# Differential heads' norm factors: from transposes in PSUM to broadcast loads through DRAM, with the normalisation moved into the forget attention

## What is computed

```python
def rmsnorm(x, g):
    xf = x.astype(jnp.float32)
    y = xf * lax.rsqrt(jnp.mean(xf * xf, axis=-1, keepdims=True) + EPS)
    return (y * g.astype(jnp.float32)).astype(x.dtype)
...
        ad = pd[:, :, 0] - lam * pd[:, :, 1]
        od = jnp.einsum('bhqk,bkhe->bqhe', ad.astype(dv.dtype), dv)
        od = rmsnorm(od, subln_g) * (1.0 - lambda_init)
        sf = jnp.einsum('bqhd,bkhd->bhqk', qf, fk).astype(jnp.float32) * (FOX_HEAD_DIM ** -0.5)
        sf = sf + jnp.transpose(cq, (0, 2, 1))[..., :, None] - cum_k[..., None, :]
        pf = jax.nn.softmax(jnp.where(causal, sf, NEG), axis=-1)
        of = jnp.einsum('bhqk,bkhd->bqhd', pf.astype(fv.dtype), fv)
        return jnp.concatenate([od.reshape(B, Q_BLOCK, DIFF_WIDTH),
                                of.reshape(B, Q_BLOCK, FOX_WIDTH)], axis=-1)
```

## Time and profile before

| | us |
|---|---|
| median of three runs | 1284.31 |
| the profiled execution's own time | 1284.02 |
| its span | 1282.2 |
| TensorE busy | 1268.9 (99%) |
| VectorE busy | 766.5 (60%) |
| ScalarE busy | 549.3 (43%) |
| GpSimd busy | 32.5 (3%) |
| chain that ended last | TensorE 95%, VectorE 3%, ScalarE 1%, issue 1% |

### The profile page before, as it was taken

The page is one execution under the profiler, slowest core; times in us unless marked ns, Lnnn a source line. Parts: engine busy times, 40 slices in busy tenths (PEclk is TensorE's granted clock), DMA queues, the critical chain, the costliest instruction groups (busy, mean ns, idle before and its releaser), DMA issues.

```text
span 1282.2 us, 17439 instructions
## 1 busy us (share of the span) xinstructions
PE 1268.9 (99%) x6386; PEld 1072.7 (84%) x6386; DVE 766.5 (60%) x1250; ACT 549.3 (43%) x921; POOL 32.5 (3%) x42
## 2 busy tenths in 40 slices
PE   9999999999999999999999999999999999999997
PEld 7887888988888888888888888888988888888886
DVE  6777895655444443323685896898868422455334
ACT  6656865433222223232564655667443222222221
POOL 0010000000000000000000000000000000000002
PEclk9999999999999999999999999999999999999999
DMA  5232113122223223332333323423122322222332
GB/s 199 85 130 83 34 36 130 34 76 89 98 98 98 98 90 124 102 111 98 99 104 110 99 83 93 114 79 112 50 66 85 112 92 92 96 98 98 99 99 82
DMA packets 37563, 120.97 MB, mean 94 GB/s; under 512 B 4600, under 2 KB 6776, under 8 KB 37504
## 3 DMA queue, kind: packets, MB, share of 16 engines
q1 hardware_dynamic: 35888, 116.93, 28.3%
q0 software_dynamic: 896, 2.64, 0.7%
q10 hardware_dynamic: 720, 0.59, 0.1%
HBM read 112.79 MB, written 2.11 MB: 90 GB/s over the span
## 4 chain that ended last, share of the span: by engine, by line
PE 95%; DVE 3%; ACT 1%; issue 1%; DVEq 0%; ACTq 0%
PE bank L902 29%; PE bank L903 29%; PE bank L904 29%; PE bank L1003 2%; PE bank L1096 1%; DVE arena L2157 1%; PE bank L1423 1%; PE bank L1125 0%; PE bank L1141 0%; PE bank L1383 0%; PE bank L1382 0%; DVE tiles L2154 0%; PE bank L1033 0%; PE bank L1073 0%; DVE tiles L2157 0%
## 5 line engine op out<-in xcount | busy, mean ns | idle before, releaser
L2154 DVE TENSOR_TENSOR w_lo<-raw_slab,w_hi 128x1024 fp32r<-128x1024 f32 (+1 forms) x199 | 243.6, 1224 | 269.1 <-ACT w_hi L1541 264.6
L902 PE MATMUL bank<-u_hi,w_hi 128*128 128x512 f32 x824 | 322.8, 392 | 0.0
L904 PE MATMUL bank<-u_hi,w_lo 128*128 128x512 f32 x824 | 321.0, 390 | 0.0
L903 PE MATMUL bank<-u_lo,w_hi 128*128 128x512 f32 x824 | 320.9, 389 | 0.0
L1541 ACT ACTIVATE w_hi<-raw_slab 128x1024 fp32r<-128x1024 f32 x197 | 207.7, 1054 | 183.8 <-PE bank L904 181.3
L902 PE MATMUL bank<-arena,w_hi 128*128 128x512 f32 (+1 forms) x692 | 260.9, 377 | 0.0
L903 PE MATMUL bank<-arena,w_hi 128*128 128x512 f32 (+1 forms) x692 | 259.3, 375 | 0.0
L904 PE MATMUL bank<-arena,w_lo 128*128 128x512 f32 (+1 forms) x692 | 259.3, 375 | 0.0
L904 PEld LDWEIGHTS bank<-u_hi,w_lo 128*128 128x128 f32 x824 | 154.7, 188 | 32.4
L902 PEld LDWEIGHTS bank<-u_hi,w_hi 128*128 128x128 f32 x824 | 154.7, 188 | 31.7 <-issue 0.9
L903 PEld LDWEIGHTS bank<-u_lo,w_hi 128*128 128x128 f32 x824 | 154.8, 188 | 30.7
(11 more groups left out here) (275 smaller groups left out, 1451.5 us busy)
## 6 DMA issues: line engine op xcount, KB each, us to landing
raw_slab<-in_stream SPq DMA_DIRECT2D x197, 512.0 KB, 3.3
aside_raw<-in_stream SPq DMA_DIRECT2D x8, 512.0 KB, 5.2
arena<-arena SPq DMA_DIRECT2D x32, 128.0 KB, 2.3
residual<-in_xT SPq DMA_DIRECT2D x8, 256.0 KB, 5.6
out_hT<-residual SPq DMA_DIRECT2D x12, 128.0 KB, 1.8
arena<-forget_rows SPq DMA_DIRECT2D x8, 128.0 KB, 2.4
raw_slab<-in_stream SPq DMA_DIRECT2D x2, 256.0 KB, 3.3
early<-decay_rows POOLq DMA_DIRECT2D x2, 256.0 KB, 3.8
```

Of the source, the lines that this page charges most:

```text
L902: pe.matmul(o, ws[0], xs[0], start=first, stop=False)
L903: pe.matmul(o, ws[0], xs[1], start=False, stop=False)
L904: return pe.matmul(o, ws[1], xs[0], start=False, stop=last)
L2154: return nc.vector.tensor_tensor(o, a, b, op)
```

## The change

One transpose of the whole 128x16 tile of factors by the identity gives 16x128 in bank 0 (`df_factor_rows`), after k-step 3 and no longer after k-step 4. ScalarE copies the rows to SBUF and stores them in DRAM (`factor_rows`, 8 KB), splits a slab, waits for the store, and issues four loads that each bring one head's row of 512 factors into all 128 partitions (256 KB each, into the tiles `MO`+h, free there). The normalisations, the high parts and the low parts leave the place between the slabs and go to the heads' work of the forget attention: `df_normed(h)` in step 6+h, ScalarE's `df_mix_hi(h)` in step 7+h, `mix_low` of head h in step 8+h. The normalisation works in place in `kept`, and so no longer waits for a temporary tile.

```diff
-DF_SPREAD_BANKS = (0, 1, 5, 7)
+DF_ROWS_BANK, DF_NORMED = 0, 6
...
+    use("df_rows", DF_ROWS_BANK, (sem.spread_ready, n + 1), (sem.df_rows, 1))
...
-            def df_spreads():
-
+            def df_factor_rows():
+
+                o = claim("df_rows")
                 pe.wait_ge(sem.rstd_done, NORM_NO["df"] + 1)
-                for h in range(DF_H):
-                    head_spread("df", h, sem.df_spread)
+                every = rstds[:, RSTD0["df"]:RSTD0["df"] + DF_H].rearrange("p h n -> p (h n)")
+                pe.transpose(o[0:DF_H * ST, 0:P], every, ident).then_inc(sem.spread_ready, 1)
...
-                    elif k == 4:
-                        df_spreads()
+                    elif k == 3:
+                        df_factor_rows()
...
+            rows = tiles[0:DF_H * ST, SQ, 0:P]
+            nc.scalar.activation(rows, full(act, "df_rows")[0:DF_H * ST, 0:P], ACT.Copy).then_inc(sem.df_rows, 1)
+            act.wait_ge(sem.df_rows, 1)
+            act.dma_start(factor_rows.rearrange("h (n p) -> (h n) p", p=P), rows).then_inc(sem.df_rows_stored, 16)
             slab_hi(SLAB0["fv"] + 2)
+            act.wait_ge(sem.df_rows_stored, 16)
             for h in range(DF_H):
+                act.dma_start(t(MO + h), factor_rows[h].partition_broadcast(P)).then_inc(sem.df_factors_loaded, 16)
+            slab_hi(SLAB0["fv"] + 3)
+
+            def df_mix_hi(h):
                 act.wait_ge(sem.head_normed, ML_H + h + 1)
-                nc.scalar.activation(ar(MIX_HI + h), t(TMP + h % 2), ACT.Copy).then_inc(sem.mix_hi, 1)
-            slab_hi(SLAB0["fv"] + 3)
+                nc.scalar.activation(ar(MIX_HI + h), kept[:, h], ACT.Copy).then_inc(sem.mix_hi, 1)
...
+                if 0 <= step - DF_NORMED - 1 < DF_H:
+                    df_mix_hi(step - DF_NORMED - 1)
...
+            slab_lo(SLAB0["fv"] + 3)
+
             def df_normed(h):
-                factor = full(dve, ("spread", f"df{h}"))
-                stt(t(TMP + h % 2), kept[:, h], sub_gain[:, 0:1], factor[:, :], ALU.mult, ALU.mult).then_inc(sem.head_normed, 1)
...
+                dve.wait_ge(sem.df_factors_loaded, 16 * DF_H)
+                stt(kept[:, h], kept[:, h], sub_gain[:, 0:1], t(MO + h), ALU.mult, ALU.mult).then_inc(sem.head_normed, 1)
...
+                h = step - DF_NORMED
+                if 0 <= h < DF_H:
+                    df_normed(h)
+                if 2 <= h < DF_H + 2:
+                    mix_low(HEAD0["df"] + h - 2, slice(0, P), h - 2, kept[:, h - 2])
```

More of the change, by code:

```diff
@@ L428, in plan_psum @@
         use(f"fv{t}", (2, 6, 3, 4)[t], slab("fv", 3), split(f"fv{t}"))
-    for h in range(DF_H):
-        filled = (sem.spread_ready, n + 1) if h == DF_H - 1 else (sem.df_spread, h + 1)
-        use(("spread", f"df{h}"), DF_SPREAD_BANKS[h], filled, (sem.head_normed, ML_H + h + 1))
+    use("df_rows", DF_ROWS_BANK, (sem.spread_ready, n + 1), (sem.df_rows, 1))
     attention("fx")
@@ L577, in __init__ @@
         self.group_done = new("group_done")
-        self.df_spread = new("df_spread")
+        self.df_rows = new("df_rows")
+        self.df_rows_stored = new("df_rows_stored")
+        self.df_factors_loaded = new("df_factors_loaded")
         self.df_stat = new("df_stat")
@@ L588, in build @@
     scratch = nc.dram_tensor("bias_rows", [DF_H, S], F32, kind="Internal").ap()
+    factor_rows = nc.dram_tensor("factor_rows", [DF_H, S], F32, kind="Internal").ap()
     decay_rows = nc.dram_tensor("decay_rows", [ML_H, S], F32, kind="Internal").ap()
@@ L1187, in head_stats, with ml_spread @@
                     last.then_inc(sem.stat_ready if h == 3 else done, 1)
-            def head_spread(name, h, done):
-                o = claim(("spread", f"{name}{h}"))
+            def ml_spread(h):
+                o = claim(("spread", f"ml{h}"))
                 for i in range(ST):
-                    factor = rstds[:, RSTD0[name] + h, i:i + 1].to_broadcast([P, P])
+                    factor = rstds[:, RSTD0["ml"] + h, i:i + 1].to_broadcast([P, P])
                     last = pe.transpose(o[:, i * P:(i + 1) * P], factor, ident)
-                last.then_inc(sem.spread_ready if h == 3 else done, 1)
+                last.then_inc(sem.spread_ready if h == ML_H - 1 else sem.ml_spread, 1)
             def rank(n):
@@ L1224, in first_fill @@
                         pe.wait_ge(sem.rstd_done, NORM_NO["ml"] + 1)
-                    head_spread("ml", int(key[6]), sem.ml_spread)
+                    ml_spread(int(key[6]))
                 elif key[:4] == "out1":
@@ L2866, in _ @@
             slab_lo(SLAB0["fv"] + 2)
+            slab_lo(SLAB0["fv"] + 3)
             def df_normed(h):
-                factor = full(dve, ("spread", f"df{h}"))
-                stt(t(TMP + h % 2), kept[:, h], sub_gain[:, 0:1], factor[:, :], ALU.mult, ALU.mult).then_inc(sem.head_normed, 1)
-            df_normed(0)
-            df_normed(1)
-            for h in range(DF_H):
-                mix_low(HEAD0["df"] + h, slice(0, P), h, t(TMP + h % 2))
-                if h + 2 < DF_H:
-                    dve.wait_ge(sem.mix_lo, HEAD0["df"] + h + 1)
-                    df_normed(h + 2)
-            slab_lo(SLAB0["fv"] + 3)
+                dve.wait_ge(sem.df_factors_loaded, 16 * DF_H)
+                stt(kept[:, h], kept[:, h], sub_gain[:, 0:1], t(MO + h), ALU.mult, ALU.mult).then_inc(sem.head_normed, 1)
             def fx_value_lo(i):
```

## The result

The changed kernel takes 1291.49 us (median of 6 runs, 1290.37 to 1292.63), the kernel before beside it 1284.25 (6 runs, 1283.98 to 1285.01): ratio 1.0054, 95% interval 1.0044 to 1.0063. It is slower by 7.2 us. The forecast was 4.6 us slower, with a range up to 1291.3; the median lies 0.2 us above that range.

A forecast was written before the change was run, and what follows sets the result against it. TensorE, busy 1268.9 of 1282.2 us, was taken as the bound, with VectorE balanced within half a microsecond in the tight steps. 1284.31 - 1.6 + 3.9 + 2.3 = 1288.9 us, range 1285.5 to 1291.3.

The forecast's parts named there:

- The signs named: Profile after: TensorE's probsT waits near 4 us, no VectorE wait before fills of steps 8 and 12, late slab stopping ScalarE.
- TensorE's gain, 1.6 us: Near 803 to 805 us: sixteen transposes go, one new one comes; 1.6 us gained, bounds 1.45 and 1.65.
- VectorE's loss, 3.9 us: Forget attention steps 6 to 11: 5.08 us of added VectorE work, partly absorbed, delays TensorE 3.9 us; bounds 0 and 5.1.
- The transfers, 2.3 us: Before the forget attention: added loads delay a weight slab, stopping ScalarE in step 0 for 2.3 us; bounds 0 and 2.7.
- I take +3.5: Weight slab issued at 807.46: its landing, normally 3.3 us after issue, was put 3.5 us later.
- The 1.2 us free of cost: Slab landing at 810.8, change at 812.0: the first 1.2 us of its delay would not stop ScalarE.
- The upper bound of 2.7: ScalarE's stop in step 0: at most 3.9 us of slab delay less 1.2 free, 2.7 us.
- the engines' free 12%: Transfer engines 88% busy from 804.5 to 810.5: the free share takes 0.7 of the added MB's 4.6 us.
- rival C: Transfers hold the slab back the full 4.6 us, 3.4 of stop, ScalarE's copies cost 0.5: 1290.5 us; chance 0.15.
- The nearest row that I took, at 86 us: Slab issued among four broadcasts of the same size took 5.7 us instead of 3.3, +2.4; basis for the landing estimate.
- their leaving gives nothing: Between the slabs before the attention: removing VectorE's and ScalarE's eight instructions gains nothing, since both waited there anyway.
- ScalarE's copies at nothing: Forget attention: ScalarE's four moved copies of 0.64 us cost nothing; without its waits for VectorE's maxima, up to 2.5 us.

The follow-up runs named there:

- e5: Kernel before plus the change's eight VectorE instructions at the same places of the forget attention, results unused: 1289.15 us against 1284.76, ratio 1.0035.
- e1: Changed kernel with the four factor loads issued from SyncE's queue, right behind the held-up weight slab, not from ScalarE's: 1286.95 us against 1284.58, ratio 1.0020.
- e6: Changed kernel with the weight slab issued after the forget rows of heads 0 and 1, ahead of heads 2 to 7: 1287.21 us against 1284.76, ratio 1.0019.
- e2: Changed kernel with VectorE's eight instructions in steps 6 to 11 given to GpSimd as twelve, loads unchanged: 1288.90 us against 1284.58, ratio 1.0033.
- e3: Changed kernel with both the factor loads issued behind the slab and VectorE's eight instructions given to GpSimd: 1288.19 us, ratio 1.0028.
- e7: Changed kernel with the slab among the forget rows and the four normalisations moved ahead of the attention on VectorE: 1290.13 us against 1284.76, ratio 1.0040.
- e4: Kernel before plus the store and four broadcast loads from ScalarE's queue, data unused, all 16 transposes kept: 1285.37 us against 1284.58, ratio 1.0006.

## Why the prediction was right or wrong

- **Slower, and from both causes named, VectorE's tight steps and the late slab: right.** e5 has the first alone (4.4 us slower), e1 and e6 take the second away. The signs named came too: TensorE's waits for probsT add up to 4.2 us, there is no wait before the fills, and the slab stops ScalarE. TensorE's wait of 2.81 us in step 2 is how that stop reached it.
- **TensorE's gain, 1.6 us: right** (1.61 at the first score). In step 7 of e1 and e6 TensorE is at -0.96, that is -1.6 and the +0.67 forecast for VectorE less 0.03.
- **VectorE's loss, 3.9 us: right, also in its course.** Forecast were 0.67, 2.0, 3.7 and 3.9 us late in steps 7, 9, 11 and 15; the same instructions in the kernel before gave 0.67, 1.92, 3.65 and 4.17. The sum of what is added less what VectorE had waited for, carried from one meeting of the engines to the next, was good to 0.3 us. The 0.3 came between steps 11 and 15, where I followed no row. In e5 VectorE reaches the fill of step 12 3.90 us late (845.05 against 840.25, each from its zero), as forecast, and then waits for ScalarE's high parts, for which it did not wait before (timeline of e5):

```profile
847.36 1.71 DVE L2157 SCALAR_TENSOR_TENSOR arena<-tiles,arena 64x512 fp32r<-64x512 f32 x2 [0.30 <-ACT arena L1558]
```

  The changed kernel has the same 0.30 us at 849.84.
- **The transfers, 2.3 us: right in kind, too small; this is the term that failed.** "I take +3.5" for the slab's landing: it was +5.3 (3.3 to 8.6). The 1.2 us free of cost were right, and 5.3 - 1.2 = 4.1 is the stop. The upper bound of 2.7 failed as well. I had let the added MB run at 229 GB/s and credited the engines' free 12% of six microseconds. The engines did more, and still had no room; the window of the whole collision in the changed kernel:

```profile
805.40:817.00 11.60, 10.84 (x51) 8.73 (x49) 1.52 (x2) 2.55 (x3) 0.00 (x0) 1.00 1.00 246
```

  A DMA share of 1.00 at 246 GB/s for 11.6 us: forget rows, factors and the slab were one pile, and the slab was at its end. Its own queue moved less than the other while both had work, from 807 to 813 us (packets, MB, share of the engines' time):

```profile
q10 hardware_dynamic: 501, 0.91, 72.6%
q1 hardware_dynamic: 288, 0.48, 30.2%
```

  q10 carries the factors, q1 rows and slabs. The Trainium skill's rule that the prediction quotes, turns between the queues packet by packet, pointed to rival C, whose 3.4 us of stop were nearer than my 2.3, and still 0.7 short. Even turns in the packets of the profile are not what the trace shows, 501 to 288; why the factors' queue got more stays open. The landing of the forget rows rose from 2.4 to 5.6 us (median), which is what the slab had ahead of it. An estimate from the trace: by the slab's issue at 808.4 q1 had moved 0.47 of the rows' 1.05 MB, and q10 0.30 of 1.05 MB. What was left of both and the slab's own 0.52 MB are 1.86 MB, 7.6 us at 246 GB/s; it took 8.6. The nearest row that I took, at 86 us, had no such queue ahead of the slab.

  One step I overlooked: "their leaving gives nothing". VectorE, rid of the eight instructions, splits the last slab of the values earlier, and so the next slab's slot is free earlier. SyncE's issues of the late slab and the next one, before and after (duration in ns, first to last start):

```profile
L740 SPq DMA_DIRECT2D raw_slab<-in_stream x2: 333/462/592, 807.5 to 811.3; - x2
...
L741 SPq DMA_DIRECT2D raw_slab<-in_stream x2: 333/460/586, 808.4 to 809.8; - x2
```

  The next slab follows after 1.4 us in place of 3.8. From 814 to 817 us q1 moved 0.92 MB, and the late slab has only 0.52, so the next one moved up to 0.4 MB before the late one had landed. That this is the us that the estimate lacks is argued; no run held the next slab back alone.
- **ScalarE's copies at nothing:** from step 3 to step 15 no wait of TensorE for ScalarE shows; right.
- **The whole.** In the profiled runs -1.6 + 4.1 + 4.2 = 6.7 us answers for the 6.66 in step 15; 0.88 us of the 7.65 between the two profiled executions lie ahead of the change's place and 0.1 behind step 15. The medians differ by 7.2 us; 0.5 of that is within the interval (5.7 to 8.1 us) and not assigned. One candidate is the clock: over the six runs of the changed kernel the mean granted clock goes from 0.998 to 0.995, and the slowest run (1292.63) has the 0.995, but only one execution has a trace. Had the transfers been put at 4.1, the forecast would have been 1290.7.

## What to carry to other kernels

Moving work to "later, where there is room" needs two rows, not one: the idle time in the very step that receives it, and the moment when its input lands. Where two in-order engines were balanced within half a microsecond, nearly every instruction added reached the other one, even one whose result nobody reads. What a load that must land soon will take is judged from all bytes ahead of it, those left on its own queue and on any other busy queue (here 7.6 of 8.6 us); moving it a few places up the issuing queue gave back 4.3 us without changing a byte. Work that leaves an engine also brings forward what that engine releases, here the next slab's transfer.

## What the runs showed of the hardware

- **GpSimd lengthens VectorE's SBUF instructions.** A tensor_scalar of 128x512 went from 0.49 to 1.57 us, a 128x1024 subtraction from 1.22 to 1.78, beside GpSimd's 128x512 subtractions of some 1.3 us each; VectorE's low parts from PSUM kept their times. Offloading eight instructions of VectorE made the kernel 2.6 us faster where the attention stood for the slab as well (e2 against the change) and 1.2 us slower where it did not (e3 against e1); in e3's trace 1.6 us go with the clock.
- **The granted clock after a wait.** In the changed kernel TensorE stood still ahead of 819.05, and towards the end of that stop the clock fell to the lower level (1.2 GHz) (windows of the changed kernel):

```profile
818.00:819.00 1.00, 0.00 (x0) 0.00 (x0) 0.32 (x1) 1.00 (x5) 0.00 (x0) 0.88 0.00 0
819.00:820.00 1.00, 0.95 (x4) 0.95 (x4) 1.00 (x3) 0.78 (x2) 0.00 (x0) 0.50 0.00 0
...
822.00:823.00 1.00, 1.00 (x6) 0.78 (x5) 1.00 (x3) 0.55 (x2) 0.00 (x0) 0.92 0.93 324
```

  The granted clock was at the lower level until 822, and in this execution it cost nothing: step 7 waited for VectorE all the same (+3.18 us there are -1.6 + 4.1 + 0.67 with nothing left). After the waits of 1.11 and 1.52 us in steps 9 and 11 it stayed at the upper level (2.4 GHz), after the 1.85 us of e3 it fell and cost 1.6 us, after the 4.1 us of e7 it fell and cost some 2.7, because no later wait for VectorE hid it. I had not expected a stop of ScalarE to reach the clock.
- **The same bytes, two prices.** Loads issued at 801.4 cost 1.0 us (e4), at 805.2, with the attention 1.6 us earlier, 4.1 us.
